# A three-block network on one core: the residual stream and its norm roots are laid out by tokens instead of by channels

## What is computed

```python
def rms(x, g):                       # norm over the 1024 channels of a token
    return x * rsqrt(mean(x * x, -1) + 1e-6) * g

def swiglu(h):                       # f..: gate and up 1024 -> 2816, down 2816 -> 1024
    return (silu(h @ w_gate) * (h @ w_up)) @ w_down

# block 1: f10, m1, f11 (its norms are modulated from c: pre, shift and gate)
x = x + k * (1 + gate) * rms(sub(rms(x, g_pre) * (1 + scale) + shift), g_post)
# block 2: f20, m2, f21
x = x + k * rms(sub(rms(x, g_pre)), g_post)
# block 3, twice: m30, f30 and m31, f31 (no norm behind the sub-layer)
x = x + sub(rms(x, g_pre))
# k = 0.5 for a feed-forward layer, 1 for a mixer
return rms(x, g_final)
```

## Time and profile before

| what | value |
|---|---|
| median of 3 runs | 3627.2 us (3626.7 to 3627.62) |
| span of the profiled execution | 3626.8 us |
| PE busy | 3478.4 us, 96% of the span |
| PE weight loads | 2717.8 us, 75% |
| DVE, ACT, POOL busy | 1965.9, 1124.9, 153.6 us |
| nine boundaries, from the last product to the end of the next sub-layer's first two units | 360.15 us |
| weights loaded | 264 units, 1024 KB each, 4.8 us from issue to landing |

### The profile page before, as it was taken

One profiled execution on the slowest core, in us unless ns is written; L12 is line 12 of the kernel. 1 busy time (PEld: TensorE's weight loads), 2 busy tenths in 40 slices (PEclk: granted clock), 3 DMA queues, 4 the chain that ended last, 5 costly groups with the idle time before them and its releaser, 6 DMA issues. The chain is left out here.

```text
span 3626.8 us, 45721 instructions
## 1 busy us (share of the span) xinstructions
PE 3478.4 (96%) x18518; PEld 2717.8 (75%) x18518; DVE 1965.9 (54%) x2658; ACT 1124.9 (31%) x1482; POOL 153.6 (4%) x127
## 2 busy tenths in 40 slices
PE   9999999999999999998799999999999999999998
PEld 7887776688878887677578886666788866568886
DVE  6667545622344333988553435795534358953334
ACT  2222334422232223342332223335322233542222
POOL 0000000000000000000000000330000022200000
PEclk7999999999999999999899999999999999999999
DMA  6554231122222222210022222210222221112221
GB/s 244 185 183 172 81 108 40 55 104 93 93 81 94 103 93 102 75 65 4 13 82 93 99 98 78 74 70 24 89 96 93 98 88 70 47 47 93 99 98 70
DMA packets 47231, 325.75 MB, mean 90 GB/s; under 512 B 5232, under 2 KB 5488, under 8 KB 8688
## 3 DMA queue, kind: packets, MB, share of 16 engines
q1 hardware_dynamic: 41792, 290.10, 22.4%
q0 software_dynamic: 5296, 33.61, 2.6%
HBM read 321.59 MB, written 2.10 MB: 89 GB/s over the span
## 5 line engine op out<-in xcount | busy, mean ns | idle before, releaser
L2107 PE MATMUL PS<-HH,WH 128*128 128x512 f32 x2264 | 895.5, 396 | 21.5 <-DVE HL L2531 15.9
L2108 PE MATMUL PS<-HL,WH 128*128 128x512 f32 x2264 | 884.1, 391 | 0.0
L2109 PE MATMUL PS<-HH,WL 128*128 128x512 f32 x2264 | 884.1, 391 | 0.0
L2513 DVE TENSOR_TENSOR WL<-RAW,WH 128x2048 fp32r<-128x2048 f32 x264 | 613.6, 2324 | 497.8 <-ACT WH L2366 497.5
L2366 ACT ACTIVATE WH<-RAW 128x2048 fp32r<-128x2048 f32 x264 | 503.0, 1905 | 297.4 <-PE PS L2109 289.5
L2107 PEld LDWEIGHTS PS<-HH,WH 128*128 128x128 f32 x2264 | 426.6, 188 | 140.3 <-issue 33.7
L2109 PEld LDWEIGHTS PS<-HH,WL 128*128 128x128 f32 x2264 | 426.6, 188 | 90.2
L2108 PEld LDWEIGHTS PS<-HL,WH 128*128 128x128 f32 x2264 | 427.0, 189 | 87.6 <-issue 1.4
L2107 PE MATMUL PS<-AH,WH 128*128 128x512 f32 x1056 | 412.5, 391 | 3.3 <-DVE A L2579 3.0
L2108 PE MATMUL PS<-AL,WH 128*128 128x512 f32 x1056 | 411.7, 390 | 0.0
L2109 PE MATMUL PS<-AH,WL 128*128 128x512 f32 x1056 | 411.5, 390 | 0.0
(11 more groups left out here) (412 smaller groups left out, 3596.7 us busy)
## 6 DMA issues: line engine op xcount, KB each, us to landing
RAW<-in_w SPq DMA_DIRECT2D x264, 1024.0 KB, 4.8
E<-in_ada POOLq DMA_DIRECT2D x28, 1024.0 KB, 5.1
E<-in_ada SPq DMA_DIRECT2D x4, 1024.0 KB, 12.0
G<-in_ada SPq DMA_DIRECT2D x4, 1024.0 KB, 20.3
X<-in_x SPq DMA_DIRECT2D x1, 2048.0 KB, 14.1
out_x<-A SPq DMA_DIRECT2D x8, 256.0 KB, 2.1
G<-in_cos POOLq DMA_DIRECT2D x4, 256.0 KB, 3.4
G<-in_sin POOLq DMA_DIRECT2D x4, 256.0 KB, 3.6
```

Source lines behind the costliest of these rows:

```text
L2107: nc.tensor.matmul(out, wh, xh, start=start, stop=False)
L2108: nc.tensor.matmul(out, wh, xl, start=False, stop=False)
L2109: return nc.tensor.matmul(out, wl, xh, start=False, stop=stop)
L2513: nc.vector.tensor_tensor(WL[:, w % 2, :], RAW[:, w % 2, :], WH[:, w % 2, :].bitcast(F32), ALU.subtract).then_inc(w_lo, 1)
```

## The change

The residual is kept token-major: `XT[p, t, d]` has 128 tokens on the partitions, four token blocks t, and the 1024 channels in a row. The sum over channels of a token block is then an instruction that squares and adds along the row (`accum_out`), and the root is one column, `ST[:, 16 t + n]`, of 128 values. Channel gains become full rows (`GAINS`): for f20, m2, f21 and the end POOL loads them; for f10, m1 and f11, where they are computed, PE spreads them (`gain_rows`) and ACT copies them out (`gains`, ahead of the sub-layer's first own work on ACT).

The down and out products exchange their operands: the activation halves are loaded as weights, 128 tokens at a time, and the weight unit streams 512 wide (`part`). Block i ends in the banks PS[2i] and PS[2i+1]. The last two units go block after block (`leave`), so that block 0 is complete 36 products ahead of the last one, block 1 24 and block 2 12. Then PE transposes the normed blocks (`turn_tokens`, eight transposes each), and the next sub-layer's first two units are multiplied in two halves of 256 tokens (`enter`): 1,680 products of 128x256 instead of 840 of 128x512. `keep_clock`, `deferred`, `entry` and the scaling of every gate and up bank are gone. The banks of the mixers are renamed (PM). In m2, `variance 3` comes ahead of `out 0` on DVE, and the out product begins with chunks 4 to 7. The output is written as four pieces of 512 KB.

```diff
+            def part(src, w, i, tokens, begins, ends):
+                wh, wl = (x[:, w % 2, :].rearrange("p (k c) -> p k c", k=2) for x in (WH, WL))
+                for c in range(2):
+                    for n, (xh, xl) in enumerate(src):
+                        last = mm3(PS[2 * i + c][:], xh[:, tokens], xl[:, tokens], wh[:, n, c * S:(c + 1) * S],
+                                   wl[:, n, c * S:(c + 1) * S], begins and n == 0, ends and n == 1)
...
+                for i in range(NT):
+                    last = one(0, i)
+                last.then_inc(w_used, 1)
+                second_arrives()
+                for i in range(NT):
+                    last = one(1, i)
+                last.then_inc(w_used, 1)
+                if onward:
+                    block_used(1, post)
+                    turn_tokens(0)
+                    turn_tokens(1)
+            def enter(s):
...
+                for half in range(2):
+                    cols_ = slice(256 * half, 256 * half + 256)
+                    for n, banks in enumerate(units):
+                        if half == 0:
+                            unit_arrives(w + n)
+                            block_used(2 + n, post)
...
+                        for k in range(KD):
+                            if n == 0:
+                                pe.wait_ge(hl_done, t("hl") + KD * half + k + 1)
...
+                            if half == 0 and n == 1 and k in (4, 6):
+                                turn_tokens(k // 2)
...
+                if s in MADE:
+                    gain_rows(s, (PS[1], PS[2]) if plan["subs"][s]["kind"] == "mix1" else (PS[0], PS[1]))
...
+                def square_out(i):
+                    for c in range(2):
+                        out_wait(act, t, 2 * i + c)
+                        nc.scalar.activation(JUNK[0][:, c * S:(c + 1) * S], PS[2 * i + c][:], ACT.Square,
+                                             accum_out=stat(i, c)).then_inc(sqh_done, 1)
...
+                def square_in(i):
+                    act.wait_ge(x_done, t("x") + i + 1)
+                    nc.scalar.activation(JUNK[1], XT[:, i, :], ACT.Square, accum_out=stat(i, 8)).then_inc(sqx_done, 1)
...
+                def gained(i):
...
+                        nc.vector.scalar_tensor_tensor(HG[:, i, c * S:(c + 1) * S], PS[2 * i + c][:], factor, GAINS[s][c],
+                                                       ALU.mult, ALU.mult).then_inc(hg_done, 1)
...
+                    nc.vector.scalar_tensor_tensor(XT[:, i, :], HG[:, i, :], root, XT[:, i, :], ALU.mult, ALU.add).then_inc(x_done, 1)
...
-            def keep_clock(n):
-                for _ in range(n):
-                    nc.tensor.matmul(PS[4 + (t("norms") + 1) % 2][:], ONES[:], CN[:, 0:S], start=True, stop=True)
...
-            for m in range(KD):
-                sp.wait_ge(t_ready if plan["final"] else x_done, final + (m + 1 if plan["final"] else KD))
-                sp.dma_start(T["out"][m * P:(m + 1) * P, :], (Y if plan["final"] else X)[:, m, :]).then_inc(stored, 16)
+            for i in range(NT):
+                sp.wait_ge(out_ready, 2 * i + 2)
+                sp.dma_start(T["out"][i * P:(i + 1) * P, :], HG[:, i, :]).then_inc(stored, 16)
```

More of the change, by code:

```diff
@@ L590, in pe_mix1 @@
             w = t("w")
[L591 to L597, removed]
             j = 1
@@ L646, in done @@
                 act.wait_ge(w_used, w + n + 1)
+            h["gains"](1)
             done(0)
-            chain(nc.scalar.activation(F1, PS[0][0:8, :], ACT.Identity, bias=PV[0:8, cols["fox_b"]:cols["fox_b"] + 1]))
+            chain(nc.scalar.activation(F1, PM[0][0:8, :], ACT.Identity, bias=PV[0:8, cols["fox_b"]:cols["fox_b"] + 1]))
             nc.scalar.activation(F2, F1, ACT.Abs).then_inc(proj_evac, 1)
@@ L1360, in pe_mix2 @@
             mm = nc.tensor.matmul
-            t.add("hl", KD)
-            for u in range(U2):
+            for u in range(2, U2):
                 h["unit_arrives"](w + u)
@@ L2020, in dve_mix2 @@
             root("a")
+            variance(3, "b", 0)
             out(0, "a", 0)
             out(1, "a", 1)
-            variance(3, "b", 0)
+            dve.wait_ge(silu2, 4)
+            for m in range(4, KD):
+                lo(m)
             out(2, "a", 2)
@@ L2430, in high_act @@
                         .then_inc(ah_done, 1)
+                if s in MADE and s:
+                    gains(s)
                 for u in (0, 1):
@@ L2470, in _ @@
             split(1)
+            high(Y, plan["subs"][0]["shift"])
+            t.add("hl", KD)
             for s, sub in enumerate(plan["subs"]):
-                if not deferred(s):
-                    high(Y, sub["shift"])
                 if sub["kind"] == "ffn":
@@ L2476, in _ @@
                 else:
-                    act_mixers[sub["kind"]](act, t, sub, dict(split=split, rsqrt=rsqrt, chain=chain, high=high))
+                    act_mixers[sub["kind"]](act, t, sub, dict(split=split, rsqrt=rsqrt, chain=chain, high=high, gains=gains))
                     w = t("w")
-                    for u in range(3):
+                    for u in range(2):
                         act.wait_ge(w_used, w + u + 1)
@@ L2767, in _ @@
-                out_passed(t, sub)
-                dve.wait_ge(x_done, t("x"))
+                boundary(s, sub)
+                t.add("out", 2 * NT - 1)
                 if plan["ada"] and s == 0:
@@ L2973, in launch_parts @@
          for n, x in arrays.items()}
-    T["out"] = nc.dram_tensor("out_x", (D, S), F32, kind="ExternalOutput").ap()
-    kinds = [s["kind"] for s in plan["subs"]]
-    n = len(kinds)
+    T["out"] = nc.dram_tensor("out_x", (S, D), F32, kind="ExternalOutput").ap()
     T["cols"], T["cncols"] = cols, cncols
-    whole = sum(k == "mix1" or k != "ffn" or sub["shift"] is not None for k, sub in zip(kinds, plan["subs"]))
-    T["final_reads"] = KD * (whole + kinds.count("mix1")) if plan["final"] else KD * (n - 1)
     build_program(nc, T, plan)
```

830 lines of the change are left out of this document (454 added, 376 removed).

## The result

The changed kernel takes 3696.5 us (median of 4 runs, 3696.34 to 3700.67), the kernel before 3627.0 us in the same comparison: ratio 1.0197, 95% interval 1.0183 to 1.0212. It is 70 us slower. The direction was forecast (3646 us), the size was not, and the time lies 12 us above the range, whose upper end is 3684.

The account below looks back on a forecast made before the run. PE, busy 3478.4 of 3626.8 us, was taken to bound the kernel, mostly with 512-column products. The terms summed to +18.3 on 3627.2 us, giving 3645.5, rounded 3646 us; range 3608 to 3684.

Parts of the forecast that it names:

- a price per product: Rival: 256-wide boundary products cost 0.14 (+25, 3671 us; 0.18 shared with costlier chains) or 0.227 (+145, 3791 us; 0.02).
- nine boundaries, without clock: Windows from a sub-layer's last product through the next one's first two units: 359.5 us against 360.15, -0.6.
- clock within them: PE's low clock after idling: 2.8 us each for f10-m1 and m1-f11, 1.7 for each block 3 boundary.
- inside m1 (gains, clock): Behind m1's first two units PE idles 7.5 us for gains made on PE, plus 2.8 of low clock.
- inside f11 (gains, clock): Behind f11's first two units PE idles 8.0 us for gains made on PE, plus 2.8 of low clock.
- f10 up to its last product: PE's 8 gain-spreading products stand within a full stream in f10, at 0.11 us each: +0.9.
- m2 between its boundaries: In m2's tail DVE's `variance 3`, put ahead of the outs, comes 4.6 us sooner: -4.6.
- down starts: Blocks 0 and 1 of a down product start without waiting for the last gated tile: -3.0 in all.
- end: From the last product to the end of the kernel takes 9.2 us instead of 15.4: -6.2.
- short columns: Rival: one-column chain instructions at boundaries are shorter: 3630 us (0.20, shared with clock up) or near 3618 (0.20, or both together).
- The clock term: Without fillers PE's clock drops after idling, at the gain waits and five of nine boundaries: +16.3 in all.
- The two stretches behind the gains: PE's idling behind the first two units of m1 and f11 while ACT copies gains: 7.5 and 8.0 us.

Follow-up runs that it names:

- a1_line40: The changed kernel with the unused tile LINE 40 instead of 8 columns wide, activation tiles 128 bytes later: 3639.0 us, ratio 1.0037 to the kernel before.
- a5_fillers: The changed kernel with LINE 40 wide, ACT's gain copies one step later, and five filler products at every boundary, five more where a norm stands: 3631.2 us, ratio 1.0013.
- a2: The changed kernel with LINE 72 instead of 8 columns wide, activation tiles 256 bytes later: 3699.3 us, ratio 1.0199 to the kernel before.
- b1: The kernel before with LINE 104 instead of 8 columns wide, activation tiles 384 bytes later: 3692.4 us, ratio 1.0181.
- b4: The kernel before with 32 unused columns ahead of X and LINE 40 wide, weights at 0 and activations at 128 modulo 256; its time is not in the text.
- b2: The kernel before with 32 unused columns ahead of X, so every tile starts 128 bytes later; its time is not in the text.
- b8: The kernel before with 32 unused columns ahead of and behind WL, so WL alone moves 128 bytes modulo 256: 3677.0 us, ratio 1.0142.

## Why the prediction was wrong

**The step that failed** stands in its first paragraph: that the products in a stream start 0.227 us apart, that the change leaves their number alone, and so leaves their time alone. The runs showed 0.233 us in its place, in a stream whose instructions are the same, and a cost of 57.5 us between the medians of the changed kernel and a1_line40 (59 between the profiled spans). The prediction took the distance of the earlier trace rows as a property of the instruction. It depends on where its operands lie, and taking four vectors out of PV moved one of them. No rival had a cause that reaches every product; the nearest, a price per product, was put on the narrow ones, which kept 0.120. The profile could not have told; the list of tiles could have raised the question, since a tile called LINE that nobody uses stood there.

**The rest**, read in a1_line40 against before (+8.6 us by the profiled spans, +13 by the comparison of medians, +18.3 forecast; the rows are rounded):

```text
term                                   forecast   measured
nine boundaries, without clock          -0.6       +1.0 (361.1, clock within)
clock within them                      +10.7        -
inside m1 (gains, clock)               +10.3      +10.2
inside f11 (gains, clock)              +10.8      +11.4
f10 up to its last product              +0.9       -4.8
m2 between its boundaries               -4.6       -2.9
m30, m31                                 0         +0.6
down starts (f20, f21, f30, f31)        -3.0       -4.0
end                                     -6.2       -2.8
sum                                    +18.3       +8.7
```

- The boundary worked out instruction by instruction was right to 1 us where there is a norm (41.6 against 42.3) and right where a shift and the low clock are added (49.4 and 49.7, against 46.4 and 47.1 plus 2.8 each). In block 3 it is 31.8 to 32.1 against 32.2; the 1.7 us of clock added there were wrong. The columns of the chain cost 0.15 to 0.30 us each, so *short columns* fell too. Three small sums of the recorded text don't come out, and none changes the forecast by more than 0.2 us: its boundaries add up to 359.3 and not 359.5, its end to 9.1 and not 9.2, and its steps of block 0 to 7.8 us, which ends at T-0.4 and not at T-0.9. What it gives for other distances of narrow products (8 us less at 0.113, 25 and 145 more at 0.14 and 0.227) is less than 1,680 times the difference (12, 34 and 180), and it does not say what hides the rest.
- The clock term is the one most over-sized. The clock does fall: PEclk is 0.75 in the window of f10-m1 above, and 0.88 at f20-m2, where the products after the wait of 5.3 us stand 0.21 apart and PEclk is 0.50 (1509.56 to 1513.20 us). But at f20-m2 PE then waits for low halves anyway, and in block 3, behind waits of 2.9 us in a1_line40, PEclk is 0.95 to 1.00. The Trainium skill ("TensorE: Matmul & The Clock Gate", section "Why this matters for your kernels") asks to avoid idle gaps of PE between bursts of matmuls, since they bring the clock back to its low level. These windows agree. Filling the gaps made the kernel slower all the same (a5_fillers), since what fills a gap also stands in PE's queue.
- The two stretches behind the gains were right to 1 us. Nothing about them is in the trace of before; they came from reading what stands ahead of a split in ACT's queue.
- f10 is the term with the wrong sign. Before, PE waited 6.2 us there for DVE's sums of the conditioning weights (L2663), and behind the wait ten products stood 0.43 apart, at the low clock (PEclk 0.50 from 314.73 to 319.16 us). After, three of four token blocks of the first down unit go ahead of that point, 36 products where 12 stood, and the wait is 0.4. Of this a new wait takes back 2.5: PE's spreading of the gains (L2206) waits for DVE to have computed them. The first line is of before, the others of after:

```profile
PE PS L2193 <- DVE E L2663: 6.2, 1, 6.2
PE PS L2199 <- DVE E L2859: 0.4, 1, 0.4
PE PS L2206 <- DVE ST L2706: 2.5, 1, 2.5
```

- m2's variance step gives the 4.6 us: the wait for it fell from 12.9 to 8.3. Two of them are lost elsewhere, in a new wait that the prediction did not have: 13 us into m2 PE stops for DVE. First the line of before, then two of after:

```profile
PE PS L1583 <- DVE A L1925: 12.9, 1, 12.9
PE PS L1598 <- DVE A L1940: 8.3, 1, 8.3
PE PS L2136 <- DVE A L1848: 2.0, 1, 2.0
```

  In a1_line40 the same stop ends at 1525.78. The first two units end at 1512.58. DVE then does 13 steps of the convolution in one run and begins the split of the next weights 10.2 us after that end, where before it began 5.1 us after it. L1848, which the trace of after names as what PE waits for, comes behind the split (the trace of a1_line40 names ACT's split, which ends within 0.1 us of it). This is read from the order of the rows; no run tests it.

```profile
1512.63 10.20 DVE L1353 SCALAR_TENSOR_TENSOR A<-A,PV 128x512 f32<-128x512 f32 x13
...
1522.75 2.28 DVE L2637 TENSOR_TENSOR WL<-RAW,WH 128x2048 fp32r<-128x2048 f32 x1
...
1524.95 0.68 DVE L1848 TENSOR_TENSOR A<-PS,SG 128x512 f32<-128x512 f32 x1
```

- The end: 12.6 us from the last product instead of 9.2. In a1_line40 DVE is still busy with block 1's final norm when the product ends at 3622.8, and adds blocks 2 and 3 only after it:

```profile
3623.49 1.42 DVE L2786 SCALAR_TENSOR_TENSOR A<-X,ST,R 128x512 f32<-128x512 f32 x2
3624.82 2.00 DVE L2761 TENSOR_TENSOR X<-X,PS 128x512 f32<-128x512 f32 x3
3626.74 0.68 DVE L2761 TENSOR_TENSOR X<-X,PS 128x512 f32<-128x512 f32 x1
```

So the token-major layout as it was meant, with the address mended, is 0.4% slower than the kernel before. That is the direction forecast and about half of the size by the profiled spans: the waits on gains, the boundaries with a norm and the down starts came as forecast, the clock in block 3, f10, m2 and the end did not. That the sum is no further off is in part luck: f10 is 5.7 us better than forecast, m2 and the end together 5.1 worse. The other 60 us are the address.

## What to carry to other kernels

Before taking the time of an untouched stream as fixed, compare the addresses of its operands in both programs: a small tile that grows or shrinks moves all behind it. Where a stream like this one is the bound, keep weights and activations at the same start modulo 256 bytes, and give tiles of odd sizes a place behind the large ones. For a queue that carries both a stage's own chain and the next weights, write down what stands ahead of each split; that gave most waits here to 1 us, though not the new one in m2, and moving one step behind a split gave 8 us.

## What the runs showed of the hardware

- Streams of 128x512 products of the rounded halves, each with its own weight load, start 0.2270 us apart when weights and activations start alike modulo 256 bytes, and 0.2325 to 0.2330 when they are 128 bytes off (after, a2, b1, and b4 with the weights at 0), and moving both together changes nothing (b2); 64 bytes off cost 1.0% of this kernel's time where 128 cost 1.8 to 1.9%. With only one of the two weight tiles off, two of three stretches are slow in most products (b8). PEclk of the window 3400 to 3600 us is 1.00 in all of them, and 128x256 products keep 0.120 (after, a1).
- An `accum_out` on ACT is an instruction of its own, 0.19 us, that overlaps the square ahead of it by 0.1 (a1_line40: the square at 3620.98 takes 1.06, the read starts at 3621.94).
- A product of the constant tile with the tile of ones, both float32, runs as two records: five of them are x10 and 7.06 us behind a wait (a5_fillers).
